# In-projections of the mixers: one full-precision fp32 product in place of three products of split fp32 halves

## The reference

```python
h = rms_norm(x, attn_norm[l])
proj = h @ w_in[l]                       # first block, both layers: 1024 x 3200
a_q, a_k, a_v, b_q, b_k, b_v, c_q, c_ff, c_fb, c_v, c_g = split_columns(proj)
o_a = gqa_attention(...)                 # 6 heads, rope
o_b = diff_attention(...)                # 4 heads, two score maps each
o_c = rms_norm(gated_linear_scan(forward) + gated_linear_scan(backward)) * silu(c_g)
x = x + concatenate([o_a, o_b, o_c]) @ w_out[l]
x = x + (gelu(depthwise_conv(norm(x) @ w_gate)) * (norm(x) @ w_val)) @ w_down[l]

# second block
u = silu(layer_norm(causal_conv31(val * sigmoid(gate))))        # even mixer, h @ w_in: 1024 x 1792
x = x + concatenate([u, banded_attention(q, k, v, sinks)]) @ w_out
att = merge(dilated attention at 1, 4 and 16)                   # odd mixer, h @ w_in: 1024 x 2048
x = x + concatenate([att, multiscale_pool(u)]) @ w_out
# two swiglu feed-forward nets per layer, each added with weight 0.5
```

## Time and profile before

| | us |
|---|---|
| three runs | 1887.75, 1887.93, 1890.23 (median 1887.93) |
| span of the profiled execution | 1882.6 |
| median less that span | 5.3 |

### The profile page before, as it was taken

One profiled execution on the slowest core, in us unless ns is written; L12 is line 12 of the kernel. 1 busy time (PEld: TensorE's weight loads), 2 busy tenths in 40 slices (PEclk: granted clock), 3 DMA queues, 4 the chain that ended last, 5 costly groups with the idle time before them and its releaser, 6 DMA issues. The chain is left out here.

```text
span 1882.6 us, 35550 instructions
## 1 busy us (share of the span) xinstructions
PE 1712.7 (91%) x13260; PEld 1625.1 (86%) x13260; DVE 1230.0 (65%) x1750; ACT 860.1 (46%) x1250; POOL 495.1 (26%) x511
## 2 busy tenths in 40 slices
PE   5887799999977999999999456999999999789999
PEld 5775799998856999999999435999999998579999
DVE  7677666657786766655557986655555556865553
ACT  3445355533543555444444243544354434435442
POOL 3040333310211433223320002333123311343320
PEclk9987899999986999999999757999999999899999
DMA  6330256644320556656654301566455654235563
GB/s 223 101 112 23 90 170 178 222 161 135 102 67 23 159 179 194 198 164 179 196 200 135 101 1 56 177 182 215 164 168 180 212 179 145 67 101 179 179 214 99
DMA packets 70800, 274.25 MB, mean 146 GB/s; under 512 B 7872, under 2 KB 9024, under 8 KB 70592
## 3 DMA queue, kind: packets, MB, share of 16 engines
q1 hardware_dynamic: 70272, 271.04, 46.3%
q0 software_dynamic: 448, 2.13, 0.3%
HBM read 272.09 MB, written 1.05 MB: 145 GB/s over the span
## 5 line engine op out<-in xcount | busy, mean ns | idle before, releaser
L744 DVE TENSOR_TENSOR wl<-raw,wh 128x1024 fp32r<-128x1024 f32 (+1 forms) x474 | 632.5, 1335 | 299.5 <-ACT wh L504 298.7
L1130 PE MATMUL gb<-hh,wh 128*128 128x256 f32 x2768 | 802.4, 290 | 26.3 <-DVE wl L744 17.0
L1131 PE MATMUL gb<-hl,wh 128*128 128x256 f32 x2768 | 788.6, 285 | 0.0
L1132 PE MATMUL gb<-hh,wl 128*128 128x256 f32 x2768 | 787.9, 285 | 0.0
L504 ACT ACTIVATE wh<-raw 128x1024 fp32r<-128x1024 f32 (+1 forms) x474 | 528.5, 1118 | 343.7 <-PE gb L1132 339.6
L1130 PEld LDWEIGHTS gb<-hh,wh 128*128 128x128 f32 x2768 | 536.6, 194 | 41.6 <-DVE wl L744 17.0
L1131 PEld LDWEIGHTS gb<-hl,wh 128*128 128x128 f32 x2768 | 536.9, 194 | 3.2 <-issue 2.9
L1132 PEld LDWEIGHTS gb<-hh,wl 128*128 128x128 f32 x2768 | 536.6, 194 | 0.0
L1131 PE MATMUL gb<-gul,wh 128*128 128x256 f32 x1056 | 298.7, 283 | 0.0
L1132 PE MATMUL gb<-guh,wl 128*128 128x256 f32 x1056 | 298.3, 282 | 0.0
L1130 PE MATMUL gb<-guh,wh 128*128 128x256 f32 x1056 | 296.5, 281 | 1.8 <-POOL gul L493 1.7
(11 more groups left out here) (190 smaller groups left out, 1666.5 us busy)
## 6 DMA issues: line engine op xcount, KB each, us to landing
raw<-in_wa SPq DMA_DIRECT2D x378, 512.0 KB, 3.6
raw<-in_wb SPq DMA_DIRECT2D x96, 704.0 KB, 4.1
x<-in_x SPq DMA_DIRECT2D x1, 1024.0 KB, 4.9
out_x<-x SPq DMA_DIRECT2D x8, 128.0 KB, 3.1
row<-in_row POOLq DMA_DIRECT2D x1, 836.0 KB, 10.6
tab<-in_bias SPq DMA_DIRECT2D x3, 256.0 KB, 4.4
con<-in_const POOLq DMA_DIRECT2D x1, 544.0 KB, 7.7
tab<-in_bias SPq DMA_DIRECT2D x1, 512.0 KB, 4.8
```

The lines of the kernel that those rows point to most:

```text
L744: nc.vector.tensor_tensor(wl[:, slot, 0:nt * P], raw[:, slot, 0:nt * P], wh[:, slot, 0:nt * P].bitcast(f32), ALU.subtract).then_inc(s_lo, 1)
L1130: nc.tensor.matmul(bank, a, rhs_h(k), start=start and k == 0, stop=False)
L1131: nc.tensor.matmul(bank, a, rhs_l(k), start=False, stop=False)
L1132: last = nc.tensor.matmul(bank, b, rhs_h(k), start=False, stop=stop and k == nt - 1)
```

## The change

The in-units of the mixers are no longer split. ACT writes x times the gain as plain fp32 into hf, which takes the place of hh and hl in SBUF; PE multiplies raw by hf, one fp32 product a weight tile (`whole_tiles`). ACT's L504, DVE's L744 and DVE's L761 fall away for these units. Out-units and feed-forward phases are as before. PE now reads raw itself, so SP may load unit i over an in-unit i-4 only when PE has finished that one (s_pe). The counts of s_lo, s_hi and s_hl leave the in-units out (`splits_to`, `WHOLE0`, `L0`).

```diff
@@ -111,6 +111,20 @@
     F0 = [FC * sum(not m for m in is_mix[:n]) for n in range(NPH)]
     G0 = [FC * sum(k == "ffn1" for k, _ in PHASES[:n]) for n in range(NPH)]
     Y0 = [sum(IN_UNITS.get(k, 0) for k, _ in PHASES[:n]) for n in range(NPH)]
+    WHOLE0 = [sum(IN_UNITS.get(k, 0) for k, _ in PHASES[:n + 1]) for n in range(NPH)]
+    L0 = [DC * sum(not m for m in is_mix[:n]) for n in range(NPH)]
+
+    def phase_of(i):
+        return max(n for n in range(NPH) if U0[n] <= i)
+
+    def whole(i):
+
+        n = phase_of(i)
+        return is_mix[n] and i - U0[n] < IN_UNITS[PHASES[n][0]]
+
+    def splits_to(i):
+
+        return sum(not whole(v) for v in range(i + 1))
 
     def k_tiles(i):
         n = max(n for n in range(NPH) if U0[n] <= i)
...
@@ -128,8 +142,10 @@
         wh = sb("wh", [P, RING, KD * P], r32)
         wl = sb("wl", [P, RING, KD * P], r32)
         x = sb("x", [P, DC * SEQ])
-        hh = sb("hh", [P, DC * SEQ], r32)
-        hl = sb("hl", [P, DC * SEQ], r32)
+        with ExitStack() as share:
+            hh = sb("hh", [P, DC * SEQ], r32, share)
+            hl = sb("hl", [P, DC * SEQ], r32, share)
+        hf = sb("hf", [P, 2 * DC * SEQ])
         mh = sb("mh", [P, DC * SEQ], r32)
         ml = sb("ml", [P, DC * SEQ], r32)
         prm = sb("prm", [P, NPRM])
...
@@ -345,9 +361,13 @@
             sp.dma_start(prm[:, :], prm_d).then_inc(s_prm, 16)
             na = nb = 0
 
-            def load(i, slot, src, width):
-                if not isinstance(i, int) or i >= RING:
-                    sp.wait_ge(s_lo, i - (RING - 1))
+            def load(i, slot, src, width, before=0):
+                if not isinstance(i, int):
+                    sp.wait_ge(s_lo, i - (RING - 1 + before))
+                elif i >= RING and whole(i - RING):
+                    sp.wait_ge(s_pe, i - (RING - 1))
+                elif i >= RING:
+                    sp.wait_ge(s_lo, splits_to(i - RING))
                 sp.dma_start(raw[:, slot, 0:width], src).then_inc(s_raw[slot], 16)
 
             for n, (kind, l) in enumerate(PHASES):
...
@@ -504,7 +524,7 @@
                 nc.scalar.activation(wh[:, slot, 0:nt * P], raw[:, slot, 0:nt * P], ACT.Copy).then_inc(s_hi, 1)
 
             def split_next(i):
-                if i < NU:
+                if i < NU and not whole(i):
                     split(i, i % RING, k_tiles(i), 16 * (i // RING + 1))
 
             def gain_hi(n, c):
...
@@ -518,7 +538,8 @@
                         part, at0 = slice(c * SEQ, (c + 1) * SEQ), slice(g + c, g + c + 1)
                     else:
                         part, at0 = ds(c * SEQ, SEQ), ds(c + g, 1)
-                    nc.scalar.activation(hh[:, part], x[:, part], ACT.Copy, scale=prm[:, at0]).then_inc(s_hh, 1)
+                    to = hf if is_mix[n] else hh
+                    nc.scalar.activation(to[:, part], x[:, part], ACT.Copy, scale=prm[:, at0]).then_inc(s_hh, 1)
 
             def norm(n):
                 act.wait_ge(s_ss, n + 1)
...
@@ -738,19 +759,19 @@
                 ins.then_inc(s_dch, 1)
                 dve.wait_ge(s_dch, steps[0] - 1)
 
-            def split(i, slot, nt):
-
-                dve.wait_ge(s_hi, i + 1)
+            def split(i, slot, nt, turn):
+
+                dve.wait_ge(s_hi, turn)
                 nc.vector.tensor_tensor(wl[:, slot, 0:nt * P], raw[:, slot, 0:nt * P], wh[:, slot, 0:nt * P].bitcast(f32),
                                         ALU.subtract).then_inc(s_lo, 1)
 
             def split_next(i):
-                if i < NU:
-                    split(i, i % RING, k_tiles(i))
+                if i < NU and not whole(i):
+                    split(i, i % RING, k_tiles(i), splits_to(i))
 
             def gain_lo(n, c):
 
-                if n < NPH:
+                if n < NPH and not is_mix[n]:
                     dve.wait_ge(s_hh, c + (DC * n + 1))
                     gain, g0 = norm_gain(n)
                     g = PRM[gain] + g0
...
@@ -1120,9 +1141,19 @@
 
         @block.tensor
         def _(pe):
-            def tiles(i, slot, bank, nt, rhs_h, rhs_l, start, stop, ready=None):
-
-                pe.wait_ge(s_lo, i + 1)
+            def whole_tiles(i, bank, ready=None):
+
+                slot = i % RING
+                pe.wait_ge(s_raw[slot], 16 * (i // RING + 1))
+                for k in range(DC):
+                    if ready is not None:
+                        ready(k)
+                    end = nc.tensor.matmul(bank, raw[:, slot, k * P:(k + 1) * P], mc(hf, k), start=k == 0, stop=k == DC - 1)
+                end.then_inc(s_pe, 1)
+
+            def tiles(i, slot, bank, nt, rhs_h, rhs_l, start, stop, ready=None, turn=None):
+
+                pe.wait_ge(s_lo, splits_to(i) if turn is None else turn)
                 for k in range(nt):
                     if ready is not None:
                         ready(k)
...
@@ -1143,8 +1174,11 @@
                 i = U0[n]
                 if n:
                     pe.wait_ge(s_xo, DC * n - 1)
-                tiles(i, i % RING, gb[0][:, 0:SEQ], DC, lambda k: mc(hh, k), lambda k: mc(hl, k), True, True,
-                      lambda k: pe.wait_ge(s_hl, DC * n + k + 1))
+                if is_mix[n]:
+                    whole_tiles(i, gb[0][:, 0:SEQ], lambda k: pe.wait_ge(s_hh, DC * n + k + 1))
+                else:
+                    tiles(i, i % RING, gb[0][:, 0:SEQ], DC, lambda k: mc(hh, k), lambda k: mc(hl, k), True, True,
+                          lambda k: pe.wait_ge(s_hl, L0[n] + k + 1))
                 norm(n)
 
 
...
@@ -1319,7 +1353,7 @@
                     elif u < nin:
                         if freed_by(kind, u):
                             pe.wait_ge(s_y, Y0[n] + freed_by(kind, u))
-                        tiles(i, i % RING, gb[bank_of(kind, u)][:, 0:SEQ], DC, lambda k: mc(hh, k), lambda k: mc(hl, k), True, True)
+                        whole_tiles(i, gb[bank_of(kind, u)][:, 0:SEQ])
                     for what, g in plan(kind, u):
                         do(what, g, m, n, kind, l)
                 pe.wait_ge(m["mix_lo"], MIX_OUT[kind])
```

More of the change, by code:

```diff
@@ L367, in _ @@
                             load(it * 4 + i, i % RING, AP(wa.tensor, it * (4 * P * DC * P) + (na + j) * (P * DC * P),
-                                                          [[DC * P, P], [1, DC * P]]), DC * P)
+                                                          [[DC * P, P], [1, DC * P]]), DC * P, WHOLE0[n])
                     na += 2 * FC
@@ L373, in _ @@
                             load(it * 4 + i, i % RING, AP(wb.tensor, it * (4 * P * KD * P) + (nb + j) * (P * KD * P),
-                                                          [[KD * P, P], [1, KD * P]]), KD * P)
+                                                          [[KD * P, P], [1, KD * P]]), KD * P, WHOLE0[n])
                     nb += 16
@@ L1054, in ahead @@
                             b = U + 2 * j + k + RING
-                            split(it * 4 + b, b % RING, DC)
+                            split(it * 4 + b, b % RING, DC, it * 4 + (b + 1 - WHOLE0[n]))
                     dve.wait_ge(s_pe, i + 1)
@@ L1085, in ahead @@
                         else:
-                            split(it * 4 + (b + k + RING), (b + k) % RING, KD)
+                            split(it * 4 + (b + k + RING), (b + k) % RING, KD, it * 4 + (b + k + RING + 1 - WHOLE0[n]))
                     ahead(0)
@@ L1344, in up @@
                         tiles(i, (U + 2 * j + k) % RING, gb[2 * j + k][:, 0:SEQ], DC, lambda k: mc(hh, k), lambda k: mc(hl, k),
-                              True, True)
+                              True, True, None, i + (1 - WHOLE0[n]))
                 for j in range(2):
@@ L1360, in down @@
                               lambda c: gul[:, (k * KD + c) * SEQ:(k * KD + c + 1) * SEQ], k == 0, k == 1,
-                              (lambda c: pe.wait_ge(s_gul, F + k * KD + c + 1)) if first and j == 0 else None)
+                              (lambda c: pe.wait_ge(s_gul, F + k * KD + c + 1)) if first and j == 0 else None,
+                              it * 4 + (b + 1 - WHOLE0[n]))
                 pe.wait_ge(s_gu, F + FC - 1)
```

## The result

The changed kernel takes 1896.07 us (median of five runs, 1895.05 to 1903.21) beside 1888.79 us of the kernel before (1887.75 to 1890.23): ratio 1.0054, 95% interval 1.0036 to 1.0071. Six more runs in a later comparison gave 1901.81 us, ratio 1.0078 (1.0060 to 1.0096). So the change makes the kernel slower by 0.5 to 0.8%, some 10 to 15 us; forecast were 1902 us and +14.

The account below looks back on a forecast made before the run. PE bounds the feed-forward phases, PE and DVE by turns the mixers. Terms +5 (first mix1), +9.5 (second), -6.6 (even), +5 (odd), +1.7 (first in-units) make +14.6 on the 1882.6 span; with 5.3, 1902 us, range 1883 to 1924.

Parts of the forecast that it names:

- Cost of one in-unit: PE in the mixers: 0.43 us per fp32 product, 3.46 us a unit, +0.58; 82 units, +47 us if PE never waited.
- The upper bound of 0.59: PE's fp32 product without overlap, +1.84 us a unit; rival of a slower fp32 stream, some 2018 us, chance 0.05.
- The start: First mix1: PE starts when the first weight lands, 14.04, not when it is split, 16.97; -2.9 us.
- Second mix1: PE goes on behind the level +4.6 us later, about +6 at in-unit 25, root's late load +3.6; together +9.5, then unchanged.
- Even: Even mixer, DVE-bound: dropped splits give -8.6 us, a late load leaves -6.6; waits take up PE's extra.
- Odd: Odd mixer: -1.3 us at in-unit 12, then out-units split behind PE's ends wait for loads; walked to +5.
- relief wins: Rival, last four in-units: late loads are covered and dropped DVE splits dominate; -5.4 us, 1882.5 us; chance 0.15.
- The late loads: First four out-units of each mixer: loads issue only at PE's end of an in-unit, 3.6 us more until DVE can subtract.
- The 5.3 us between span and median: Whole kernel: added to the forecast span of 1897.2 us to give a median of 1902.5 us.
- Nothing is given back: Rival: PE's extra borne in full in mix1 and odd, +39 us, even at 0; 1927 us; chance 0.14.
- The late loads are covered: Rival, last four in-units: ACT and DVE reach out-units' splits over 4.7 us after PE's end, nobody waits; 1882.5 us, chance 0.15.
- cancel: Rival: costs and gains nearly cancel, a stall or two less than counted; 1888 us; chance 0.11.

Follow-up runs that it names:

- e4: Changed kernel, but each mixer's first four out-units are loaded during its in-units into a place of their own; 1870.45 us, ratio 0.9903 to before.
- e3: Changed kernel, but PE makes three fp32r products of rounded activations per in-unit weight tile instead of the fp32 product; 1875.72 us, ratio 0.9925 to before.
- e6: Changed kernel with e3's cheap PE products and e4's early loads together; 1846.10 us, ratio 0.9785 to before.
- e9: e4, but the last of the four early loads is left late, as in the changed kernel; 1881.44 us, ratio 0.9957 to before.
- e5: e4, but ACT and DVE do unused work shaped like the in-units' splits at the same places, without waiting for loads; 1916.18 us, ratio 1.0147 to before.
- e7: The changed kernel run and profiled once more, nothing altered; 1901.81 us, ratio 1.0078 to before.

## Why the prediction was right or wrong

The sign, the size (+14.1 forecast, +7.3 and +14.4 in two comparisons) and the sign and size of three stretches came out. Two of its terms were too small, and in opposite directions, so that the total is right in part by luck.

- *Cost of one in-unit:* right. 0.432 us a product, 3.46 a unit. Only the 0.1 us of a longer first step was missing (0.1 x 82 = 8 us at most; how much of it waits cover no run shows). The Trainium skill (TensorE: Matmul & The Clock Gate, "Back-to-back issue gap") gives columns over 2.4 GHz plus 2.5 ns for a matmul by itself and says that in a stream with weight loads both set the spacing. The split products of after start 0.12 us apart as before, so the +69 us by the bare formula were no case here; they set the formula's figure for the split products against the rows' figure for the new ones.
- *The upper bound of 0.59:* excluded by the same rows; there is no slow stream.
- *The start:* PE begins at 14.63 instead of 16.97, forecast -2.9:

```profile
14.63 4.63 PE L1151 MATMUL gb<-hf,raw 128*128 128x256 f32 x10 [14.63 <-DMA raw<-in_wa]
```

  and the first norm product 1.3 us earlier. First mix1 with the start: +4.6 by the profile pair, forecast +5.
- *Second mix1:* the walk was right at both places that can be checked in the rows. PE goes on behind the level's wait at 540.99, 4.6 us later against the start of the stretch than at 531.46 (forecast +4.6). The root's reciprocal stands 9.5 us later against it (forecast +9.5), and ACT's and DVE's rows show the chain, for the earlier trace rows:

```profile
563.01 1.06 ACT L524 ACTIVATE wh<-raw 128x1024 fp32r<-128x1024 f32 x1 [2.54 <-DMA raw<-in_wa]
564.08 1.28 ACT L611 ACT_TABLE_LOAD   x1
565.38 0.69 ACT L611 ACTIVATE sq<-mb,eps 128x512 f32<-128x512 f32 x1
...
566.10 3.35 DVE L824 RECIPROCAL sq<-sq 128x512 f32<-128x512 f32 x1 [0.78 <-ACT sq L611]
```

  The forecast then said "so it stays". It doesn't: the stretch is 13.1 us longer (217.02 for 203.94 before rounding), 3.6 more. Behind the root's wait the same 32 small products take 7.09 us for 3.79, at a granted clock of 0.50 (1.2 GHz) for 1.00 (2.4 GHz). The product and its window, of after:

```profile
571.13 7.09 PE L1320 MATMUL gb<-tv,at 128*128 128x64 f32 x32
...
571.10:578.10 7.00, 7.00 (x34) 0.50 0.00 0
```

  and the same step of before:

```profile
554.38 3.79 PE L1286 MATMUL gb<-tv,at 128*128 128x64 f32 x32
...
554.40:558.20 3.80, 3.80 (x34) 1.00 0.12 46
```

  The five groups from the root's wait on, of which this is one, take 13.8 us instead of 7.3. PE's next wait for the square root takes 3.7 us of that back (0.96 us for 4.69), so PE is then 2.8 us later than the forecast has it; the last 0.8 us are not followed. The missing term is the clock. It isn't the late load's alone: in e4 the step takes 7.09 us as well. There PE comes out of the root's wait 1.3 us earlier than before, where the forecast's case has +3, and 3.5 us are lost behind it, so that the +2.3 of e4's stretch agree with the +3 by luck.
- *Even:* forecast -6.6, measured -6.3 and -6.6. Its two parts: without late loads -9.1 (forecast -8.6), the late load 2.8 (forecast 2.0), and PE's extra free (e3: +0.2, e6 against e4: 0.8).
- *Odd:* forecast +5, measured +6.0 and +5.9.
- *The relief against PE's extra:* this is the term that was mis-sized. The case "relief wins", which is this change without late loads, was put at -5.4; e4 is that case, and is faster by 18 us (ratio 0.9903), by 13.9 in the profiles. In the first mix1 with the start it is -6.7 for a forecast of -1.5, in the odd mixer -1.8 for 0; the even one fits, the second (+2.3 for +3) by luck. Which step of the first mix1's walk was too small is not shown: it was carried over from the second with a lump for the start.
- *The late loads:* 14.6 + 5.4 = 20 us forecast, 26 measured by the medians of after and e4, 29 by their ratios, 31 and 33 by after's second set of runs and by the profiles. The waits were right (6.5 in the second mix1, as forecast; e9 has the root's alone), the 4.4 us at the lower clock behind the level's wait weren't in it. The relief less PE's units was forecast 8 to 13 us too small and the late loads 6 to 13: that these two nearly cancel is luck, and it is why the sum came out.
- *The 5.3 us between span and median:* wrong as what lies around a span. That is 1.8 us; the rest was that the profiled execution was a short one. The forecast doesn't suffer by it: span, change and 5.3 together are before's median of 1887.93 and the change of 14.6.
- *Rivals.* "Nothing is given back" fell by e5: even without relief PE's extra costs 28 us, not 39, and with relief the change is far from it. "The late loads are covered" fell by e4 and e9. The first comparison's 1896 lies between "cancel" (1888) and the forecast (1902), 6 us from the forecast and 8 from the rival; the second's 1902 is the forecast's. "A stall or two less" than counted, the rival's mechanism, is not what the rows show: both of the second mix1's are there.

Stretch by stretch, from the windows of each kernel's profile:

| | PE's units | relief | late loads | mix1 | mix1 | even | odd | ratio |
|---|---|---|---|---|---|---|---|---|
| before | | | | 208.3 | 203.9 | 171.9 | 128.2 | 1 |
| e6 | | x | | 194.9 | 197.4 | 162.0 | 121.5 | 0.9785 |
| e4 | x | x | | 204.1 | 206.2 | 162.8 | 126.4 | 0.9903 |
| e3 | | x | x | 206.3 | 206.9 | 165.8 | 127.8 | 0.9925 |
| e5 | x | | | 217.5 | 209.6 | 172.7 | 134.1 | 1.0147 |
| after | x | x | x | 214.2 | 217.1 | 165.6 | 134.2 | 1.0054 |

From before over e6 and e4 to after: the relief -41 us, PE's longer units +22, the late loads +29 (ratios times 1889; the intervals are some 3 us to either side of each ratio, and the late loads are +33 with after's second set). e6's gain holds the earlier start too: its first norm product is at 19.0 us, before's at 22.2. The experiments agree in other orders: e5, with PE's units alone, is at +28, of which 1.5 are its late start, and e3 is 20 to 26 under after. Half of the relief is eaten by PE, and the late loads take more than the other half. e4 is the version that beats both kernels.

## What to carry to other kernels

When a change lets one engine skip a step, look at what that step released. Here the subtraction freed the buffer early, and without it the next load starts at the matmul's end, behind which a split in program order waits; a place of its own for four loads turned +10 us into -18 (ratios 1.0054 and 0.9903). When a wait of TensorE grows, count the instructions behind it as well, at the lower clock. And compare a profile with its own runs' spans before a difference to the median is called overhead.

## What the runs showed of the hardware

The price of a wait at the clock, not foreseen: in e4 the level's wait is short,

```profile
526.62 1.16 PE L1249 MATMUL gb<-qq,gu 64*128 64x128 f32 x16 [0.95 <-DVE qq L1001]
```

and PE's clock in the windows around it stays at 1.00 (2.4 GHz):

```profile
526.60:532.30 5.70, 4.81 (x34) 1.00 0.27 95
532.30:536.00 3.70, 3.70 (x18) 1.00 0.00 0
```

In the changed kernel the wait is 4.00 us; it is still at 1.00 during it, and behind it at 0.58 and 0.72 in the mean, between the levels (0.50 is 1.2 GHz):

```profile
536.90:541.00 4.10, 0.10 (x3) 1.00 0.35 128
541.00:549.70 8.70, 7.83 (x34) 0.58 0.01 2
549.70:554.80 5.10, 5.10 (x19) 0.72 0.00 0
```

So 3.05 us more of waiting came with 4.4 us more of work. The other traces of this place go the same way: behind e7's wait of 3.83 us the same groups take 11.8 us, behind e9's of 0.95 they take 7.69 as in e4. It is no new cost of the change, though: the kernel before waits 3.55 us here and pays it too, at 0.50 behind the wait.

```profile
527.90:531.40 3.50, 0.01 (x1) 0.89 0.24 53
531.40:540.00 8.60, 7.67 (x32) 0.50 0.32 103
```

What is new is that e4 gets it back.

A plain fp32 product of 128x128 weights and 256 columns shows as two records 0.216 us apart with 0.379 of its own length each, 0.43 us, against 3 x 0.12 = 0.36 for the three of the split one: in this stream 20% more for PE, and one instruction of DVE and one of ACT less per unit.
